# Moving the low parts of twelve weight panels from GpSimd to VectorE in a two-block transformer kernel

## The reference, cut to what matters

```
(a_q, a_k, a_v, i_q, i_k, i_w, b_q, b_kv, b_g, c_qkv, mix_g) = _split_last(h @ w_in[layer], IN_SIZES)
y_a = _dsa_attention(...) @ w_branch_a[layer]      # A: 8 heads, the top 64 keys of a query
y_b = _nsa_attention(...) @ w_branch_b[layer]      # B: 8 heads, two softmaxes each (and a compressed one)
y_c = _dilated_attention(...) @ w_branch_c[layer]  # C: 4 heads in each of three groups
g = jax.nn.sigmoid(mix_g).reshape(bsz, seq, 3, D_MODEL)
x = x + (g[:, :, 0] * y_a + g[:, :, 1] * y_b + g[:, :, 2] * y_c) @ w_out[layer]
```

## Time and profile before

| | before |
|---|---|
| median of three runs | 1124.93 us |
| the profiled execution: its own time | 1123.92 us |
| its span, first to last instruction | 1122.1 us |
| TensorE matmul busy | 1090.6 us (97%) |
| VectorE busy | 830.0 us (74%) |
| ScalarE busy | 546.8 us (49%) |
| GpSimd busy | 109.6 us (10%) |
| granted TensorE clock, mean | 0.996 |

### The profile page before, as it was taken

How to read it: one execution, slowest core, us unless ns; L and a number is a source line. 1 busy time by engine, 2 the same in 40 slices (tenths; PEclk the granted TensorE clock), 3 DMA queues, 4 the chain that set the end, 5 groups by cost and what they waited for, 6 DMA issues and landing times.

```text
span 1122.1 us, 15979 instructions
## 1 busy us (share of the span) xinstructions
PE 1090.6 (97%) x6209; PEld 903.6 (81%) x6209; DVE 830.0 (74%) x1288; ACT 546.8 (49%) x842; POOL 109.6 (10%) x94
## 2 busy tenths in 40 slices
PE   4999999999999998999999999999999999999998
PEld 2776777888888887988888898877777688888887
DVE  2678788699999888987764686678674867676753
ACT  1536236464454433544543565757565445555532
POOL 0000000000000014000000002145555000000000
PEclk9999999999999999999999999999999999999999
DMA  9988773767988775676856466434333445666563
GB/s 340 351 320 208 265 263 107 277 216 253 336 293 316 283 261 176 238 256 218 276 190 195 151 203 195 154 111 150 114 113 113 151 151 158 186 185 187 188 193 105
DMA packets 145020, 236.91 MB, mean 211 GB/s; under 512 B 4901, under 2 KB 86322, under 8 KB 144690
## 3 DMA queue, kind: packets, MB, share of 16 engines
q1 hardware_dynamic: 138128, 221.12, 59.2%
q10 hardware_dynamic: 6818, 14.78, 4.2%
HBM read 229.33 MB, written 6.55 MB: 210 GB/s over the span
## 4 chain that ended last, share of the span: by engine, by line
PE 87%; DVE 7%; ACT 2%; issue 2%; POOL 1%; ACTq 1%; DMA 0%; POOLq 0%; DVEq 0%
PE bank L699 83%; PE bank L841 3%; DVE ring_lo L1970 1%; POOL ring_lo L2940 1%; ACTq L1573 1%; ACT w_hi L1539 1%; PE bank L900 1%; DMA big<-in_ln_b 0%; DVE small L2310 0%; DVE small L2781 0%; DVE aux L2763 0%; DVE aux L2837 0%; ACT h L1548 0%; DVE y_tok L2840 0%; DVE y_tok L2308 0%
## 5 line engine op out<-in xcount | busy, mean ns | idle before, releaser
L1970 DVE TENSOR_TENSOR ring_lo<-ring,w_hi 128x1024 fp32r<-128x1024 f32 (+4 forms) x290 | 337.4, 1198 | 135.8 <-ACT w_hi L1539 135.3
L1539 ACT ACTIVATE w_hi<-ring 128x1024 fp32r<-128x1024 f32 (+3 forms) x312 | 314.2, 1039 | 249.3 <-PE bank L699 219.4
L699 PE MATMUL bank<-h,w_hi 128*128 128x512 f32 (+1 forms) x1152 | 364.5, 380 | 0.1
L699 PE MATMUL bank<-h,ring_lo 128*128 128x256 f32 x1056 | 281.8, 281 | 0.0
L699 PEld LDWEIGHTS bank<-h,w_hi 128*128 128x128 f32 x1152 | 204.3, 189 | 46.0 <-issue 2.2
L699 PE MATMUL bank<-w_hi,h 128*128 128x512 f32 (+4 forms) x640 | 191.4, 383 | 3.3 <-ACT big L1825 2.2
L699 PEld LDWEIGHTS bank<-h,ring_lo 128*128 128x128 f32 x1056 | 193.2, 189 | 0.5 <-issue 0.5
L699 PEld LDWEIGHTS bank<-w_hi,h 128*128 128x128 f32 x640 | 118.5, 188 | 26.8 <-issue 4.8
L699 PE MATMUL bank<-ring_lo,h 128*128 128x512 f32 (+4 forms) x320 | 115.0, 379 | 0.0
L699 PE MATMUL bank<-w_hi,ff_hi 128*128 128x512 f32 x264 | 103.2, 391 | 0.0
L699 PE MATMUL bank<-w_hi,ff_lo 128*128 128x512 f32 x264 | 102.7, 389 | 0.0
(11 more groups left out here) (276 smaller groups left out, 1342.8 us busy)
## 6 DMA issues: line engine op xcount, KB each, us to landing
aux<-in_w_mod SPq DMA_DIRECT2D x24, 2048.0 KB, 9.4
ring<-in_ffn_w_in SPq DMA_DIRECT2D x88, 512.0 KB, 5.0
ring<-in_w_in SPq DMA_DIRECT2D x24, 1024.0 KB, 5.0
ring<-in_ffn_w_out SPq DMA_DIRECT2D x22, 1024.0 KB, 5.3
ring<-in_w_ffn_in SPq DMA_DIRECT2D x44, 512.0 KB, 4.8
ring<-in_attn_w_qkv SPq DMA_DIRECT2D x12, 1024.0 KB, 12.0
ring<-in_w_ffn_out SPq DMA_DIRECT2D x11, 1024.0 KB, 5.1
bias_rows<-srow ACTq DMA_DIRECT2D x1, 5376.0 KB
```

Source lines behind the costliest of these rows:

```text
L699: return nc.tensor.matmul(o, l, r, start=start, stop=stop, **kw)
L1539: nc.scalar.activation(half_of(i, 0, half), raw_half(i, half), ACT.Copy).then_inc(w_hi, 1)
L1970: V.tensor_tensor(half_of(i, 1, half), raw_half(i, half), half_of(i, 0, half).bitcast(F32), ALU.subtract).then_inc(w_lo, 1)
```

## The change

`lo_by_pool`, `mix_lo` and the semaphore `w_lo_mix` go. `split_lo` on VectorE makes the low part of every split panel, so those of the twelve mixing panels fall at the places of `next_low`, and `wait_lo` has one form.

```diff
-        lo_by_pool = [key[0] == "mix" for key, *_ in panels]
...
-        by_dve = [sum(not lo_by_pool[j] for j in split_panels if j <= i) for i in range(len(panels))]
-        by_pool = [sum(lo_by_pool[j] for j in split_panels if j <= i) for i in range(len(panels))]
+        by_dve = [sum(j <= i for j in split_panels) for i in range(len(panels))]
...
         def wait_lo(eng, i, half=1):
 
-            if lo_by_pool[i]:
-                eng.wait_ge(w_lo_mix, by_pool[i])
-            else:
-                eng.wait_ge(w_lo, 2 * by_dve[i] - 1 + half)
+            eng.wait_ge(w_lo, 2 * by_dve[i] - 1 + half)
...
             def split_lo(i):
 
-                if not lo_by_pool[i]:
-                    if i == 0:
...
-                    for half in range(2):
-                        wait_hi(dve, i, half)
-                        V.tensor_tensor(half_of(i, 1, half), raw_half(i, half), half_of(i, 0, half).bitcast(F32),
-                                        ALU.subtract).then_inc(w_lo, 1)
+                if i == 0:
...
+                for half in range(2):
+                    wait_hi(dve, i, half)
+                    V.tensor_tensor(half_of(i, 1, half), raw_half(i, half), half_of(i, 0, half).bitcast(F32),
+                                    ALU.subtract).then_inc(w_lo, 1)
...
-            def mix_lo(i):
-
-                if lo_by_pool[i]:
-                    for c in range(panels[i][2]):
-                        if c % 2 == 0:
-                            wait_hi(pool, i, c // 2)
-                        ins = nc.gpsimd.tensor_tensor(panel_part(i, 1)[:, c, :], raw_panel(i)[:, c, :],
-                                                      panel_part(i, 0)[:, c, :].bitcast(F32), ALU.subtract)
-                    ins.then_inc(w_lo_mix, 1)
-
-            split_to = splitter(mix_lo)
-
...
-            split_to(len(panels) - 1)
```

More of the change, by code:

```diff
@@ L332, in build @@
         w_used = sem("w_used")
-        w_hi, w_lo, w_lo_mix, h_hi = sem("w_hi_by_act"), sem("w_lo_by_dve"), sem("mix_lo_by_pool"), sem("h_hi_done")
+        w_hi, w_lo, h_hi = sem("w_hi_by_act"), sem("w_lo_by_dve"), sem("h_hi_done")
         odd_whole = sem("odd_chunks_whole")
@@ L1962, in split_lo @@
             def split_lo(i):
-                if not lo_by_pool[i]:
-                    if i == 0:
-                        wait_landed(dve, 0)
-                        V.tensor_copy(panel_part(0, 0), raw_panel(0)).then_inc(w_hi_first, 1)
-                    for half in range(2):
-                        wait_hi(dve, i, half)
-                        V.tensor_tensor(half_of(i, 1, half), raw_half(i, half), half_of(i, 0, half).bitcast(F32),
-                                        ALU.subtract).then_inc(w_lo, 1)
+                if i == 0:
+                    wait_landed(dve, 0)
+                    V.tensor_copy(panel_part(0, 0), raw_panel(0)).then_inc(w_hi_first, 1)
+                for half in range(2):
+                    wait_hi(dve, i, half)
+                    V.tensor_tensor(half_of(i, 1, half), raw_half(i, half), half_of(i, 0, half).bitcast(F32),
+                                    ALU.subtract).then_inc(w_lo, 1)
             split_to = splitter(split_lo)
```

## The result

| | before | changed |
|---|---|---|
| median, 13 runs each on one chip | 1124.81 us | 1127.64 us |
| ratio changed/before | | 1.0023, 95% interval 1.0015 to 1.0031 |
| the profiled execution: its own time, its span | 1123.92, 1122.1 us | 1127.82, 1125.8 us |

The change costs 2.6 us (0.0023 x 1124.8; 1.7 to 3.5 by the interval). It is slower, by about 0.2%; whether by more than 0.2% (2.2 us) the interval leaves open. The forecast had +1.5 us, which lies just under the interval, and "within 0.2%" as the likeliest case; the time, 1127.64 us, lies in its range. One execution of the changed kernel took 2179.51 us; it was disturbed and is left out of the ratio.

A forecast was written before the change was run, and what follows sets the result against it. TensorE was taken to bound the kernel: +2.1 us of new wait at mixing panel 8 less 0.55 us at panel 10 gave +1.5 us, 1126.4 us on the median of 1124.93. The range was 1124.1 to 1129.2 us.

The forecast's parts named there:

- within 0.2%: Whole kernel: the time would differ from before by less than 0.2% (2.2 us); chance 0.69.
- The bound: Stage of the mixing panels, 760 to 859 us: TensorE, busy 98.0 of 99 us, sets the pace; only its waits count.
- What is removed, -0.55 us: Mixing panel 10: TensorE's wait for GpSimd goes, -0.55 us; GpSimd's other work there held nobody up.
- What is added, 2.27 us a low part: VectorE in the mixing stage: each of twelve low parts takes 2.27 us of its time, 27 us in all.
- What VectorE gets back, 2.2 us: VectorE's SBUF-only instructions shorten without GpSimd: 1.6 us up to turn 7, 0.6 more in turn 8.
- the slower rival: VectorE gets nothing back and becomes the bound; panel 8 is 4.3 us late, +3.8 us, 1128.7 us; chance 0.29.
- Lateness gathers from 763 us on, every gap is eaten: VectorE from 763.2 us: low parts use up 11.8 us of gaps; panel 7 is in time, panel 8 2.1 us late.
- No wait elsewhere: Mixing stage: apart from panel 8, no panel stalls TensorE; VectorE catches up behind it, and panel 10 has no wait.
- The sum, +1.5 us: Whole kernel: +2.1 us waiting at panel 8 less 0.55 at panel 10, giving 1126.4 us.
- The rival of the other side, hidden: VectorE's logits and weighing pack 2 us tighter in 68; panel 8 is in time, -0.5 us, 1124.4 us; chance 0.14.

The follow-up runs named there:

- Experiment 1: Kernel before, edited so GpSimd makes the low parts of mixing panels 1 to 6 only and VectorE those of 7 to 12: 1127.49 us, ratio 1.0029.
- experiment 2: Kernel before, edited so GpSimd makes mixing panel 7's low part alone and VectorE the other eleven: 1124.00 us, ratio 0.9997.
- experiment 6: Changed kernel with seven unused 128 x 128 matmuls on TensorE ahead of mixing panel 8: 1126.22 us, ratio 1.0012.
- experiments 4: Changed kernel with mixing panel 8's low part ahead of the logits of unit 11 on VectorE, not behind them: 1125.14 us, ratio 1.0004.
- 5: Changed kernel with 14 unused 128 x 128 matmuls on TensorE ahead of mixing panel 8: 1127.37 us, ratio 1.0024.
- 8: Changed kernel with the mask of 128 x 1024 moved from turn 8 to turn 9, behind panel 8's low part: 1124.87 us, ratio 0.9999.
- 9: The changed kernel again, unedited, against the kernel before: 1127.59 us, ratio 1.0026.
- 3: Kernel before, edited so GpSimd makes mixing panel 8's low part alone and VectorE the others: 1123.65 us, ratio 0.9996.
- 7: Kernel with only panel 8's low part by GpSimd, plus 14 unused matmuls on TensorE where there is no wait: 1127.56 us, ratio 1.0015.
- 10: Changed kernel with four unused 128 x 128 matmuls on TensorE ahead of mixing panel 8: 1125.59 us, ratio 1.0010.
- 11: Changed kernel with panel 8's low part ahead of unit 11's logits and the 128 x 1024 mask one turn later: 1124.53 us, ratio 0.9997.

## Why the prediction was right, and where not

- **The bound** (TensorE sets the pace; only its waits count): right. 24.9 us more of VectorE work and 62.6 us less of GpSimd's moved the end by 2.6 us, and the two profiles show nothing new in the stage but at panels 8 and 10 (+3.0 us).
- **What is removed, -0.55 us:** right. No wait at panel 10 in any kernel without GpSimd's set there.
- **What is added, 2.27 us a low part:** right (829.03 to 831.30).
- **What VectorE gets back, 2.2 us:** the size was right. Where the prediction had 0.72 us for L2795 and 0.99 for L2680, L2789 now takes 0.16 and L2674 0.23, and the mask of 128 x 1024 takes 1.22 for 1.77. The mask's 0.55 us comes behind the gap at 812 us and counts in full. Of the 1.66 us ahead of that gap (0.56, 0.34 and 0.76) 0.50 us are left over as the gap itself; the other 1.16 us are what brings VectorE to it in time. Had nothing come back, the wait at panel 8 would be 1.99 + 0.55 + 1.16 = 3.7 us: an estimate from these rows, which no run tests, and a little under the rival's 4.3. Experiment 1 doesn't test it either: GpSimd still lengthens those instructions there (L2796 takes 0.42 and 0.48 us at 765 and 772 us), but VectorE makes no low parts beside them and has 3.21 us of gap left. By the Trainium skill (SBUF - State Buffer, "SBUF: two separate sides"), whichever of GpSimd and such a VectorE instruction comes first holds the shared port pair for its whole instruction; the trace agrees, also in the other direction of the test: with GpSimd's panel 7 back (experiment 2) the mask is 0.6 us longer again.
- **"Lateness gathers from 763 us on, every gap is eaten":** not quite, and the argument of the slower rival leans on it. By its own sum VectorE would be 0.2 us late at the logits of unit 10 (six low parts 13.6, less 11.8 and 1.6); it was on time, with 0.50 us of gap left. Most of the difference is that instructions without a gap between them overlap a little: L2786 begins at 767.40 us, while the one ahead of it ends at 767.49, and with seven gaps closed about 0.09 us each make 0.6. The carried 0.2 is small, so the wait came out right (2.1 forecast, 1.99 measured), but the picture of 68 us without any slack was false: two turns make the wait. Of 0.1 us more in each of eight low parts, the gap would have taken 0.5 of the 0.8 us.
- **No wait elsewhere:** right. The table of waits has no other for L1964 in the stage, and VectorE's gap of 4.80 us behind panel 9 shows that it had caught up:

```profile
842.30 0.61 DVE L2757 SCALAR_TENSOR_TENSOR aux<-bank,small,aux 128x128 f32<-128x128 f32 x2 [4.80 <-PE bank L694]
```

- **The sum, +1.5 us:** short by one term. The prediction priced the 2.1 us wait at 2.1 us. The matmuls behind it cost 1.56 us more, since the granted clock fell to half. This missing term took the result from +1.5 to about 0.2%: right in mechanism and place, wrong in the price of the idle time. The range held the result because it reached up to the slower rival, whose mechanism (nothing comes back) did not occur, and not because it had this term. The trace of before had shown such a fall, at its longest wait in the middle of the program (TensorE's timeline, then the windows behind it):

```profile
447.54 3.24 PE L900 MATMUL bank<-table,y_tok 128*128 128x128 f32 x16 [3.79 <-ACT y_tok L1593]
```

```profile
448.00:452.00 4.00, 4.00 (x22) 3.85 (x21) 3.27 (x4) 2.57 (x7) 0.00 (x0) 0.57 0.97 360
```

  Behind 3.79 us of idle time the granted clock is 0.57 over four microseconds. The prediction did not look there, and read its waits by their own length alone. (The changed kernel has the same wait, and there its clock is 0.50 in this window and 0.85 in the next, against 0.57 and 1.00: the cost of a long pause differs between executions, and the 0.64 us by which that execution came late to the stage arose behind it, since this wait ends 0.36 us earlier than before.)

  But the same trace has a wait nearer in length, and behind it the clock stays full. Just ahead of the stage TensorE waits 1.79 us for ScalarE, in every kernel here. Below are that wait and the four microseconds behind it in the kernel before, then the same four in experiment 6:

```profile
753.96 0.36 PE L699 MATMUL bank<-w_hi,h 128*128 128x256 f32 x1 [1.79 <-ACT big L1825]
```

```profile
754.00:758.00 4.00, 4.00 (x38) 3.70 (x39) 3.86 (x15) 3.45 (x12) 0.00 (x0) 1.00 0.03 8
```

```profile
754.00:758.00 4.00, 4.00 (x22) 4.00 (x22) 3.83 (x15) 3.46 (x13) 0.00 (x0) 0.57 0.00 0
```

  Of the thirteen profiles, six keep clock 1.00 behind this wait (before, changed, experiments 4, 5, 8 and 9) and seven fall to 0.50 (1, 2, 3, 6, 7, 10 and 11). So from the trace of before alone the term could have been named as a risk, but not counted on.
- **The rival of the other side, hidden:** it wanted 2 us of tighter packing in 68; the overlap of instructions gave the 0.6 us above.

What stays open: whether the clock falls at panel 8 in every execution. It did in the three profiles with this wait, and in none of the ten without it; but behind the 1.79 us it fell in seven of thirteen. With it stays open how much of the difference between the sum, 3.0 us, and the measured 2.6 is noise. The interval holds both.

## What to carry to other kernels

Follow a late engine only back to its last gap in the trace of the changed kernel: what came ahead of that gap made no lateness. But ask what keeps the gap open; here it was 0.50 us wide, and time saved ahead of it was what left it there. An engine's share of work says little about a move; here 25 us went for nothing, and one place in the order, behind 4.3 us of logits, cost all of it, while the same work a step earlier cost nothing that the runs can tell (experiments 4 and 11). And when an engine that is never idle gets a new wait of microseconds, look at its clock behind the wait before giving the wait a price, and in more than one execution; here 2 us of idle time cost 3.6 us in each of three profiles.

## What the hardware showed that I had not expected

- TensorE's granted clock went to half for about 3.4 us after a pause of 1.98 to 2.03 us (two kernels, three profiles), and stayed full after pauses of 0.23, 0.32, 0.65 and 0.89 us at the same place. Elsewhere in the program, the pause of 3.79 us at 447 us is also followed by a low clock, in all thirteen profiles. The length of the pause alone doesn't settle it: behind the pause of 1.79 us at 753 us the clock fell in seven profiles and stayed full in six, and it stayed full behind one of 1.95 us at 387 us (experiment 2). What else decides, no run here shows. In short windows the clock is 0.50 or 1.00, with values between only in windows that hold the step. The Trainium skill (TensorE: Matmul & The Clock Gate, "Part 1: The HAM clock gate") says that the ratio has these two levels only (a third, 13/16, it gives for three or more busy cores of a die); the traces of this one core agree.
- At panel 8 the fall costs the same each time, 1.56, 1.57 and 1.62 us, though it begins at 830.9 us in one trace and at about 832.1 in another.
- A plain fp32 matmul of 128 x 128 takes 0.24 us and is recorded as two (28 in 3.39 us for 14 issued). I had planned with half of that.
